# Expert weight tiles loaded as two 1 MB transfers with a semaphore for each half

## The reference

```python
def hier_moe(xf, w_rg, b_rg, w_re, b_re, w1, w3, w2):
    ...
    top_v, top_i = lax.top_k(e_in, TOP_K)
    gate = jax.nn.softmax(top_v, axis=-1) * g_val
    expert = g_idx * EXPERTS_PER_GROUP + top_i
    ...
    def expert_block(args):
        xblk, e = args
        return (jax.nn.silu(xblk @ w1[e]) * (xblk @ w3[e])) @ w2[e]
    ...
    out = jnp.zeros((T + 1, D), yb.dtype).at[row_tok].add(yb * row_gate[:, None].astype(yb.dtype))
```

## Time and profile before

| what | value |
|---|---|
| median of 3 timed runs | 2412.09 us (2407.84 to 2416.21) |
| the profiled execution, its own time | 2415.46 us |
| the profiled execution, its span | 2413.6 us |
| PE busy | 2065.9 us (86%) |
| DVE, ACT, POOL busy | 708.6, 335.5, 67.1 us |
| mean granted clock of PE | 0.924 |
| moved by the DMA engines | 639.57 MB, of it 596.04 MB on SP's queue |
| first mixture, first to last expert matmul | 1194.7 to 1678.4 us |
| second mixture, first to last expert matmul | 1910.4 to 2391.9 us |

### The profile page before, as it was taken

How to read it: one execution, slowest core, us unless ns; L and a number is a source line. 1 busy time by engine, 2 the same in 40 slices (tenths; PEclk the granted TensorE clock), 3 DMA queues, 4 the chain that set the end, 5 groups by cost and what they waited for, 6 DMA issues and landing times.

```text
span 2413.6 us, 20625 instructions
## 1 busy us (share of the span) xinstructions
PE 2065.9 (86%) x8515; PEld 1097.1 (45%) x8515; DVE 708.6 (29%) x1344; ACT 335.5 (14%) x719; POOL 67.1 (3%) x81
## 2 busy tenths in 40 slices
PE   7989999898999998999697787876599687887785
PEld 4547766455577664444433333332255433333231
DVE  1236664325366553022300000000664300000001
ACT  1221101115210012000110000000234100000001
POOL 0000000001000000000000000000100100000000
PEclk9979999998999998999699989898699699999998
DMA  8526677254266673111599999999310799999995
GB/s 310 183 70 228 237 247 250 79 171 141 70 244 242 245 252 120 37 70 64 220 428 427 427 428 427 427 428 398 123 70 32 285 427 427 427 427 428 427 427 226
DMA packets 154846, 639.57 MB, mean 265 GB/s; under 512 B 16784, under 2 KB 67664, under 8 KB 130048
## 3 DMA queue, kind: packets, MB, share of 16 engines
q1 hardware_dynamic: 135328, 596.04, 62.3%
q0 software_dynamic: 10112, 25.31, 2.9%
q10 hardware_dynamic: 9312, 16.88, 1.8%
HBM read 623.38 MB, written 25.30 MB: 269 GB/s over the span
## 4 chain that ended last, share of the span: by engine, by line
PE 69%; DMA 18%; DVE 5%; issue 5%; ACT 3%; SPq 0%; POOL 0%; ACTq 0%; DVEq 0%; POOLq 0%
PE psum L474 17%; PE psum L1891 13%; PE psum L896 13%; DMA ring<-in_w 8%; PE psum L884 6%; PE psum L1909 6%; DMA normed_t<-in_w 6%; PE psum L1426 3%; DMA arena<-in_w 3%; DVE normed_t L449 1%; PE psum L1557 1%; ACT arena L1241 1%; DMA arena<-expert_outputs,row_of_choice 1%; PE psum L977 1%; PE psum L1565 1%
## 5 line engine op out<-in xcount | busy, mean ns | idle before, releaser
L1891 PE MATMUL psum<-ring,arena 128*64 128x512 f32 x1280 | 388.5, 667 | 109.8 <-issue 107.9
L474 PE MATMUL psum<-ring,normed_t 128*128 128x512 f32 (+1 forms) x864 | 354.3, 573 | 2.9 <-DMA ring<-in_ab_w_in 1.2
L896 PE MATMUL psum<-normed_t,ring 128*128 128x256 f32 x1408 | 310.4, 383 | 2.7 <-DVE normed_t L449 2.7
L1891 PEld LDWEIGHTS psum<-ring,arena 128*64 128x64 f32 x1280 | 129.4, 153 | 359.1 <-issue 359.1
L896 PEld LDWEIGHTS psum<-normed_t,ring 128*128 128x128 f32 x1408 | 270.7, 192 | 44.1 <-issue 3.8
L474 PEld LDWEIGHTS psum<-ring,normed_t 128*128 128x128 f32 x864 | 163.1, 200 | 188.7 <-issue 185.9
L2166 DVE TENSOR_TENSOR scaled<-scaled,psum 128x512 f32<-128x512 f32 x32 | 22.0, 687 | 631.3 <-PE psum L1891 631.3
L816 DVE SCALAR_TENSOR_TENSOR arena<-ring,silu_c,arena 128x1024 f32<-128x1024 f32 x168 | 204.5, 1278 | 0.0
L1909 PE MATMUL psum<-ring,consts 128*64 128x512 f32 x640 | 173.2, 600 | 26.1 <-DMA ring<-in_w 11.9
L884 PE MATMUL psum<-ring,arena 128*128 128x512 f32 x352 | 154.3, 596 | 0.0
L1891 PE MATMUL psum<-arena 128*64 128x512 f32 x512 | 123.0, 636 | 32.8 <-issue 32.8
(11 more groups left out here) (383 smaller groups left out, 1792.3 us busy)
## 6 DMA issues: line engine op xcount, KB each, us to landing
ring<-in_w SPq DMA_DIRECT2D x120, 2048.0 KB, 28.9
arena<-in_w SPq DMA_DIRECT2D x48, 2048.0 KB, 29.3
ring<-in_w_mod SPq DMA_DIRECT2D x24, 2048.0 KB, 8.3
normed_t<-in_w SPq DMA_DIRECT2D x24, 2048.0 KB, 33.1
ring<-in_ffn_w_up SPq DMA_DIRECT2D x44, 1024.0 KB, 10.0
ring<-in_ffn_w_down SPq DMA_DIRECT2D x10, 2048.0 KB, 9.2
expert_outputs<-consts ACTq DMA_DIRECT2D x64, 256.0 KB, 10.4
ring<-in_ab_w_in SPq DMA_DIRECT2D x6, 2048.0 KB, 21.3
```

What stands on the lines that cost most here:

```text
L474: m = te.eng.matmul(PS[:, bank, 0:n], src[:, k0 + k, P * t:P * t + P], w[:, k, :], start=(k == 0), stop=(k == kc - 1))
L896: m = pe.matmul(PS[:, b, 256 * hf:256 * hf + 256], w[:, hf, k, P * cc:P * cc + P], HT[:, k, 0:T], start=(k == 0), stop=(k == KC - 1))
L1891: m = pe.matmul(PS[64 * h:64 * h + 64, 2 + q, :], XT[:, c % 2, k, 64 * h:64 * h + 64], w[h][:, k, :], start=k == 0, stop=k == KC - 1)
```

## The change

Each 2 MB tile is issued as two transfers of 1 MB, u = 0 for the first 2048 of its 4096 columns and u = 1 for the rest. Each half has a semaphore of its own. In `pe_hidden` PE waits for the first halves of both tiles before block k = 0 and for the second halves before k = 4. In `pe_out` it waits for the first halves before its first matmul and for the second halves before block j = 2 of output half 0. The slots, the order of the tiles and what frees a slot stay as they were.

```diff
+        def upto(who, key):
+            return table.get((who, key), 1)
+
         def wait(eng, who, key):
-            eng.wait_ge(sems[who], table.get((who, key), 1))
+            eng.wait_ge(sems[who], upto(who, key))
...
-                self.w_loaded = [s(f"weights{i}_loaded") for i in range(MSLOTS)]
+                self.w_loaded = [[s(f"weights{i}{'ab'[u]}_loaded") for u in range(2)] for i in range(MSLOTS)]
...
-            def loaded(self, pe, c, q):
+            def loaded(self, pe, c, q, u):
                 for h in range(2):
                     n = 6 * c + 2 * q + h
-                    pe.wait_ge(self.w_loaded[n % MSLOTS], 16 * (n // MSLOTS) + 16)
+                    pe.wait_ge(self.w_loaded[n % MSLOTS][u], 16 * (n // MSLOTS) + 16)
...
-                sp.dma_start(self.slots[i], src).then_inc(self.w_loaded[i], 16)
+                for u in range(2):
+                    sp.dma_start(self.slots[i][:, 2048 * u:2048 * u + 2048], src[:, 2048 * u:2048 * u + 2048]).then_inc(self.w_loaded[i][u], 16)
...
             def pe_hidden(self, te, c, q):
-                self.loaded(pe, c, q)
+                self.loaded(pe, c, q, 0)
...
                 for k in range(KC):
+                    if k == KC // 2:
+                        self.loaded(pe, c, q, 1)
...
-                self.loaded(pe, c, 2)
+                self.loaded(pe, c, 2, 0)
...
                     for j in range(4):
+                        if (n, j) == (0, 2):
+                            self.loaded(pe, c, 2, 1)
```

More of the change, by code:

```diff
@@ L539, in ab_pe @@
                     p.step(m, f"ret.pv{g}")
-            wait(pe, "dve", "ml.rows")
+            pe.wait_ge(sems["dve"], upto("dve", "ml.rows"))
             pe.wait_ge(consts_loaded, 16)
@@ L547, in ab_pe @@
             p.step(m, "ml.colt")
-            wait(pe, "dve", "ml.mqk")
+            pe.wait_ge(sems["dve"], upto("dve", "ml.mqk"))
             for h in range(5):
@@ L575, in ab_pe @@
                     p.step(m, f"ab.ytr{j}{t}")
-            wait(pe, "dve", "ab.yt11")
+            pe.wait_ge(sems["dve"], upto("dve", "ab.yt11"))
             for n in range(2):
@@ L786, in ab_dve @@
                 for t in range(2):
-                    wait(dv, "pe", f"ab.out{n}.t{t}")
+                    dv.wait_ge(sems["pe"], upto("pe", f"ab.out{n}.t{t}"))
                     xr = X[:, t, 512 * n:512 * n + 512]
@@ L806, in mod_products @@
                     if m_ % 2 == 0 and v >= 2:
-                        wait(dv, "pe", f"mod{i}.sum{v - 2}")
+                        dv.wait_ge(sems["pe"], upto("pe", f"mod{i}.sum{v - 2}"))
                 w = W(name).rearrange("p (k n) -> p k n", k=4)[:, k, :]
@@ L831, in mod_row_dve @@
         def mod_row_dve(dv, p, i, v):
-            wait(dv, "pe", f"mod{i}.sum{v}")
+            dv.wait_ge(sems["pe"], upto("pe", f"mod{i}.sum{v}"))
             if v:
@@ L837, in mod_row_act @@
         def mod_row_act(ac, i, v):
-            wait(ac, "dve", f"mod{i}.row{v}")
+            ac.wait_ge(sems["dve"], upto("dve", f"mod{i}.row{v}"))
             for r in range(2):
@@ L989, in ple_act @@
             for t in range(2):
-                wait(ac, "pe", f"ple{i}.e.t{t}")
+                ac.wait_ge(sems["pe"], upto("pe", f"ple{i}.e.t{t}"))
                 p.settle()
@@ L1149, in nsa_pe @@
                     p.step(m, f"nsa.cpv{t}{g}")
-            wait(pe, "dve", "nsa.kt1")
+            pe.wait_ge(sems["dve"], upto("dve", "nsa.kt1"))
             n = len(HEADS2)
@@ L1398, in nsa_dve @@
                 for n in range(2):
-                    wait(dv, "pe", f"nsa.out{n}.t{t}")
+                    dv.wait_ge(sems["pe"], upto("pe", f"nsa.out{n}.t{t}"))
                     xr = X[:, t, 512 * n:512 * n + 512]
@@ L1431, in em_pe @@
             columns("b", 4, "dve")
-            wait(pe, "act", "em.a3")
+            pe.wait_ge(sems["act"], upto("act", "em.a3"))
             for n in range(9):
@@ L1500, in em_dve @@
                 for t in range(4):
-                    wait(dv, "pe", f"em.out{n}.t{t}")
+                    dv.wait_ge(sems["pe"], upto("pe", f"em.out{n}.t{t}"))
                     residual(dv, p, "em", "pe", PS[:, 4 * n + t, :], t, n, GB[:, t // 2, :], f"em.res{n}{t}", RES[:, t % 2, :])
@@ L1738, in at_dve @@
                 for n in range(2):
-                    wait(dv, "pe", f"at.out{n}.t{t}")
+                    dv.wait_ge(sems["pe"], upto("pe", f"at.out{n}.t{t}"))
                     residual(dv, p, "at", "pe", PS[:, 4 + 2 * t + n, :], t, n, GB[:, 0, :], f"at.res{n}{t}", RES[:, t % 2, :])
@@ L1834, in load_weights @@
                 elif i < 6:
-                    wait(sp, "dve", self.before)
+                    sp.wait_ge(sems["dve"], upto("dve", self.before))
                 elif i == 6:
@@ L2029, in act @@
                 ac.activation(SM[0:1, 831:832], cst("ones", 1)[:, 0:1], ACT.Copy).then_inc(self.y, 1)
-                wait(ac, "dve", L + ".over")
+                ac.wait_ge(sems["dve"], upto("dve", L + ".over"))
                 n = ac.value_load(OVF[0:1, 16:17], min_val=0, max_val=15)
@@ L2256, in _ @@
             for t in range(2):
-                wait(sp, "dve", f"moe1.x{t}" if on("out") else "end")
+                sp.wait_ge(sems["dve"], upto("dve", f"moe1.x{t}" if on("out") else "end"))
                 sp.dma_start(out[0, P * t:P * t + P, :], X[:, t, :]).then_inc(out_sem, 16)
@@ L2279, in _ @@
             if on("at"):
-                wait(po, "dve", "moe0.end")
+                po.wait_ge(sems["dve"], upto("dve", "moe0.end"))
                 gate_rows(po, 2, 1, 2)
             if on("out"):
-                wait(po, "dve", "at.res11")
+                po.wait_ge(sems["dve"], upto("dve", "at.res11"))
                 gate_rows(po, 3, 1, 5)
```

392 lines of the change are left out of this document (196 added, 196 removed).

## The result

The changed kernel takes **2421.95 us** (median of 7 runs, 2420.53 to 2424.22) and the kernel before 2412.73 us (7 runs). The ratio is 1.0039, with a 95% interval of 1.0029 to 1.0049. So the change makes the kernel slower by 9.4 us (7 to 12). The forecast was +8.4 us, 2420.5 us. The profiled execution has a span of 2419.2 us and a time of its own of 2420.96 us; against the profile before that is 5.6 us more.

What follows compares the result with a forecast made beforehand. The prediction took the DMA engines to bound the kernel in both mixtures. Rows +13.4, transfers and waits 0, tails -3.0 and -2.0 summed to +8.4 us, 2420.5 us from the median of 2412.09; range 2406 to 2429.

Steps and rivals of the forecast that it cites:

- The bound: In both mixtures the DMA engines set the pace, at a share of 1.01, and PE waits for tiles.
- The rows: Expert tiles on the path: 1408 added rows per engine at 9.5 ns each, +13.4 us (10.1 to 15.3).
- A transfer costs nothing: Second transfer of each expert tile: its start and completion add 0, at most 12 us.
- SP's issues are hidden: SP's queue: issues double at 0.43 us each; twelve per expert pair (5 us) hide under at least 29 us of transfer.
- The second waits on PE cost nothing: PE's waits for second halves in the middle of a step: 0, hidden by PE's 19% of idle time.
- The tails: Ends of the mixtures: PE starts on first halves, gaining 2.0 us in the first and 3.0 us in the second.
- The doubt about the first mixture: Behind the first mixture, gathers starting sooner find the queue fuller, so its tail was taken as -2.0 us (1.0 to 3.5).
- its signs: About 49400 packets, plateau 421 to 422 GB/s, share 1.01 or more, mixtures about 4 us longer, last w2 step starting early.
- Rival 1: Expert tile rows: 8 KB go as fast as 16 KB, leaving only the gain at the ends, 2407 us; chance 0.25.
- Rival 2: Added expert tile transfers: each costs something, 0.035 us x 176 = 6 us on top, 2427 us; chance 0.13.
- Rival 3: In the mixtures, halves shorten the plateau itself by 4.4 us, above 428 GB/s, 2403 us; chance 0.07.

Runs made afterwards that it cites:

- whole waits: Against the kernel before: two 1 MB transfers per tile, PE waiting for both halves ahead of each step; 2425.44 us, ratio 1.0046, and again 2426.16 us, ratio 1.0048.
- quarters: Against the kernel before: only the last four tiles of each layer cut, into quarters of 512 KB with a semaphore each; 2407.86 us, ratio 0.9978.
- the kernel that has rows alone: Against the kernel before: still one 2 MB transfer per tile, but two 8 KB rows per partition that can't be joined; 2423.12 us, ratio 1.0043.
- the small transfers: Against the kernel before: a transfer of 16 rows of 256 bytes added behind each tile on SP's queue; 2413.91 us, ratio 1.0006.

## Why the prediction was right

- **The bound.** The forecast took the DMA engines at a share of 1 for what sets the pace. The share stayed at 1.02, and of the profile's added 5.6 us the mixtures have 5.2. Right.
- **The rows**, +13.4 us from 9.5 ns each. Right in kind, somewhat too large: the three kernels with whole waits and 8 KB rows gave 11.1, 11.6 and 10.4 us, 11.0 on average, which is 7.8 ns over 1408 rows (35.2 us over 4224 gives 8.3). It lies within the bounds of 10.1 to 15.3. What drew the figure up was the window at 432 GB/s, 8 us long; the 450 us at 427 alone would have given 8.5 to 9.1 ns. (The prediction prints 8.6 for the lower one; (639 - 614) / 3 is 8.3, and 8.5 before rounding. Its sum does not depend on it.)
- **A transfer costs nothing.** Right: +1.4 us (-1.0 to +3.9) for 192 of them with a row for each engine. The Trainium skill gives the 2.0 us that the prediction quotes (DMA: Bandwidth & Descriptors, "Anatomy of one DMA") for transfers that GpSimd issues; these are SP's, and no run here measures that figure.
- **SP's issues are hidden.** Right in effect, but the time of an issue was wrong; see the last section.
- **The second waits on PE cost nothing.** Nothing speaks against it: PE stays at 80% busy on the same plateau, and in the last w3 steps no gap shows where the wait stands.
- **The tails**, -5.0 us. By the medians they gave back about 2 us within the change (+9.3 on average over the two measurements of the change, against +11.4 with whole waits), and each of these figures is uncertain by about 3 us. Alone, for the last four tiles, they gave 7.2, 2.2 and, with quarters, 5.3 us. So the term has the right sign and 2 to 7 us as its size. The traces tell the two mixtures apart, by the time from release to the end of w2. The changed kernel has 476.6 and 476.7 us in the first and 475.1 and 475.0 in the second; whole waits have 477.6 and 477.5 in the first and 477.8 and 478.6 in the second. The second mixture's tail thus gave about 3.2 us where 3.0 were forecast, and the first one's 0.9 where 2.0 were. In both, w3 started sooner, by 2.8 us in the first and 2.6 in the second, as the forecast's 2.45 has it. In the first mixture it then ran at the lower clock for half of its time (9.5 us, against 7.1 with whole waits) and gave most of that back; this the forecast had not reckoned with. The doubt about the first mixture was that the gathers would find the queue full and give the gain back. The spare room of the earlier trace rows did fill up, to a share of 1.01 in the same place, six microseconds from 5.5 us after the end of w2:

```profile
1688.60:1694.60 6.00, 0.00 (x0) 0.00 (x0) 0.00 (x0) 1.89 (x4) 1.47 (x2) 0.50 1.01 378
```

but from the end of w2 to the attention stage's long run of matmuls it is 1727.57 - 1683.08 = 44.5 us, against 1723.99 - 1678.45 = 45.5 us before, so nothing was given back there:

```profile
1723.99 11.18 PE psum L474 x21
```

The sum came out closer than its terms, and that is luck: rows were 2.4 us too dear, and the tails within the change some 3 us too generous by the medians (1 us by the traces). Of its signs the packets, the plateau, the share and the start of the last w2 step came true; each mixture was to be about 4 us longer, and the traces have 2.0 and 3.2.

**The rivals.** Rival 1 (8 KB go as fast as 16 KB) fell with the plateau at 421 and with the kernel that has rows alone. By the Trainium skill's rule of 3 cycles (DMA: Bandwidth & Descriptors, "Why small descriptors are slow") an added packet would cost 3.6 ns, an estimate; 7.8 to 8.3 were measured. Rival 2 (6 us for the added transfers) fell with the small transfers and with the kernel that has rows alone. Rival 3 needed more than 428 GB/s.

## What to carry to other kernels

Where the DMA engines are busy all the time, count rows (unbroken runs of one partition), not only bytes: here each row added by cutting rows of 16 KB to 8 or 4 KB cost its engine about 8 ns, and a transfer as such next to nothing. A wait by halves is worth only what stands behind the last landing; cut those few tiles and leave the rest whole, which here beats the kernel before by 2 to 7 us and the changed one by some 11 to 17. A price read from short windows with other row sizes, on both sides of the one in question, came out right to within a quarter here (9.5 ns against 7.8); the 450 us window was the better base than the one of 8 us. And what an earlier start wins at a tail can be lost again to the clock that PE is granted behind the idle time.

## What the runs showed that I had not expected

**SP waits inside its issues.** I took 0.43 us for one. In the changed kernel the issues of the expert tiles read (ns, least, median, most):

```profile
L1847 SPq DMA_DIRECT2D ring<-in_w x240: 327/2129/7030, 1039.6 to 2358.6; - x120
L1847 SPq DMA_DIRECT2D arena<-in_w x96: 328/2131/6999, 1145.0 to 2354.3; - x96
L1847 SPq DMA_DIRECT2D normed_t<-in_w x48: 429/2121/2661, 1170.9 to 2363.0; - x48
...
DMA to landing us min/median/max: 4.9/28.2/33.3
```

The median is 2.1 us, about the 2.45 us in which the engines move 1 MB. This looks like a full queue, into which a transfer gets when another is through; it was not tested by itself. Before, the medians were 0.33 to 0.43 us, and with four transfers of 512 KB they are 1.08 us. Two other kernels bear on what fills up, the one cut between partitions (twice the transfers, rows as before) and the one transfer with two rows (twice the rows, transfers as before):

```profile
L1847 SPq DMA_DIRECT2D ring<-in_w x240: 465/596/605, 1040.6 to 3135.9; - x120
...
L1841 SPq DMA_DIRECT2D ring<-in_w x120: 367/368/7942, 1038.3 to 2357.7; - x120
```

With twice the transfers no issue took over 0.62 us; with twice the rows some took up to 7.9 us, though the median stayed at 0.37. So it goes with the rows in the queue and not with the transfers. The landing times are near those before (medians 28.2 and 29.2 us), the share is 1.02, and no time is seen to be lost by it; what stood behind SP's issues was only more tiles.

**The engines do not finish together.** Windows of 2 us at the end of the second mixture, first of the kernel before, then of the changed one:

```profile
2371.00:2373.00 2.00, 0.41 (x2) 0.00 (x0) 0.00 (x0) 0.60 (x1) 0.00 (x0) 1.00 0.90 385
2374.00:2376.00 2.00, 2.00 (x12) 0.74 (x10) 0.00 (x0) 0.00 (x0) 0.00 (x0) 1.00 0.65 270
2377.00:2379.00 2.00, 2.00 (x13) 0.74 (x10) 0.00 (x0) 0.00 (x0) 0.00 (x0) 1.00 0.44 188
2380.00:2382.00 2.00, 1.18 (x7) 0.56 (x4) 0.69 (x1) 0.00 (x0) 0.00 (x0) 1.00 0.12 49
```

```profile
2380.00:2382.00 2.00, 2.00 (x6) 0.54 (x4) 0.00 (x0) 0.00 (x0) 0.00 (x0) 0.50 0.93 389
2383.00:2385.00 2.00, 2.00 (x12) 0.78 (x10) 0.00 (x0) 0.00 (x0) 0.00 (x0) 1.00 0.62 262
2386.00:2388.00 2.00, 1.94 (x10) 0.47 (x6) 0.02 (x1) 0.00 (x0) 0.00 (x0) 1.00 0.40 168
2389.00:2391.00 2.00, 1.11 (x8) 0.68 (x9) 0.00 (x0) 0.60 (x1) 0.00 (x0) 1.00 0.12 49
```

The rate falls step by step over some 9 us, while no other transfer is queued. So some engines seem to be through some 9 us, nearly two tiles' time, before the slowest, and PE waits for a tile's full count of 16, and so for the slowest. I had taken the end of the plateau as sharp. Which engines lag and why was not tried.

**64 partitions at a time** ran at 227 GB/s with a share of 1.01, as told above.
